# Decoder trunk on one core: the page loop's softmax steps set further apart, and the expert layers' first weight halves and exponentials moved earlier

## The reference

```
def page_step(carry, p_idx):
    ckv = pool_ckv[page_table[:, p_idx]]
    s = mla_scores(q_nope, q_pe, mla_keys(ckv, w_uk, kn_nope), pool_kpe[phys])
    return merge(carry, s, ckv), None          # running softmax, values = p @ ckv
```

```
q = (xb @ w_q).reshape(PEER_BLOCK, PEER_HEADS, 2, PEER_D_KEY // 2)
s = einsum('thcd,cnd->thcn', q, sub_keys)      # 8 heads, two halves, 128 keys each
s1, i1 = top_k(s[:, :, 0], 16); s2, i2 = top_k(s[:, :, 1], 16)
top_s, top_pos = top_k(s1[..., :, None] + s2[..., None, :], 16)
gate = softmax(top_s); act = gelu(u_tab[experts] . xb)
return sum(gate * act * v_tab[experts])
```

## Time and profile before

| | before |
|---|---|
| median of 3 timed runs | 3015.54 us (3010.78 to 3016.44) |
| the profiled execution's own time | 3003.13 us |
| its span in the profile | 3001.5 us |
| TensorE busy | 2789.8 us, 93% of the span |
| VectorE, ScalarE, GpSimd busy | 62%, 43%, 7% |
| mean granted TensorE clock | 0.949 of 2.4 GHz |
| query loops of the two expert layers | about 383 to 450 us, 2120 to 2187 us |
| experts | about 453 to 1252 us, 2190 us to the end |
| page loop | about 1411 to 2050 us; the first 16 pages carry the prompt's 16 heads too |

### The profile page before, as it was taken

One profiled execution on the slowest core, in us unless ns is written; L12 is line 12 of the kernel. 1 busy time (PEld: TensorE's weight loads), 2 busy tenths in 40 slices (PEclk: granted clock), 3 DMA queues, 4 the chain that ended last, 5 costly groups with the idle time before them and its releaser, 6 DMA issues.

```text
span 3001.5 us, 59707 instructions
## 1 busy us (share of the span) xinstructions
PE 2789.8 (93%) x22390; PEld 2577.9 (86%) x22390; DVE 1864.9 (62%) x3534; ACT 1292.3 (43%) x2607; POOL 221.0 (7%) x319
## 2 busy tenths in 40 slices
PE   8977899999999999976989999998999999999998
PEld 5767689999999999845877777777899999999998
DVE  5566469989975555424654444442679899855554
ACT  2333124477764444311433333331244677644443
POOL 0044000000000000000022222221000000000000
PEclk9999999999999999986989998887999999999999
DMA  4311135444445555620122222221345444455553
GB/s 165 121 35 31 60 116 168 162 157 159 157 155 182 182 180 179 220 102 14 32 71 74 73 75 66 67 62 60 122 155 164 160 156 159 146 181 181 182 181 134
DMA packets 105660, 378.50 MB, mean 126 GB/s; under 512 B 14618, under 2 KB 14875, under 8 KB 104931
## 3 DMA queue, kind: packets, MB, share of 16 engines
q1 hardware_dynamic: 88562, 322.17, 32.4%
q0 software_dynamic: 16880, 53.42, 6.0%
HBM read 371.52 MB, written 4.01 MB: 125 GB/s over the span
## 4 chain that ended last, share of the span: by engine, by line
PE 87%; DVE 8%; issue 2%; ACT 2%; DMA 0%; DVEq 0%; POOL 0%; ACTq 0%; POOLq 0%; SPq 0%
PE ps L733 85%; DVE arena L1929 2%; DVE arena L1374 1%; ACT arena L2072 1%; DVE arena L1378 1%; PE ps L1032 1%; PE ps L1027 1%; DVE arena L1958 0%; DVE ring_lo L1374 0%; PE ps L792 0%; DVE arena L1951 0%; DVE arena L1939 0%; ACT w_hi L2072 0%; DVE arena L1932 0%; DVE arena L1892 0%
## 5 line engine op out<-in xcount | busy, mean ns | idle before, releaser
L1374 DVE TENSOR_TENSOR ring_lo<-ring,w_hi 128x1024 fp32r<-128x1024 f32 x512 | 625.4, 1223 | 418.0 <-ACT w_hi L2072 413.5
L2072 ACT ACTIVATE arena<-ps 128x256 f32<-128x256 f32 (+18 forms) x981 | 396.9, 424 | 964.5 <-PE ps L733 886.4
L2072 ACT ACTIVATE w_hi<-ring 128x1024 fp32r<-128x1024 f32 x512 | 541.8, 1059 | 391.4 <-PE ps L733 391.1
L733 PE MATMUL ps<-x_hi,w_hi 128*128 128x264 f32 x2048 | 595.5, 291 | 15.5 <-DVE ring_lo L1374 15.5
L733 PE MATMUL ps<-h_hi,w_hi 128*128 128x264 f32 x2048 | 580.5, 283 | 6.8 <-DVE ring_lo L1374 6.8
L733 PE MATMUL ps<-x_hi,ring_lo 128*128 128x264 f32 x2048 | 585.0, 286 | 0.0
L733 PE MATMUL ps<-x_lo,w_hi 128*128 128x264 f32 x2048 | 584.8, 286 | 0.0
L733 PE MATMUL ps<-h_lo,w_hi 128*128 128x264 f32 x2048 | 582.7, 285 | 0.0
L733 PE MATMUL ps<-h_hi,ring_lo 128*128 128x264 f32 x2048 | 582.3, 284 | 0.0
L733 PEld LDWEIGHTS ps<-arena 64*64 64x64 f32 (+4 forms) x5452 | 440.8, 160 | 157.3 <-DVEq L1371 45.4
L733 PE MATMUL ps<-arena 64*64 64x64 f32 (+11 forms) x5452 | 483.0, 252 | 89.1 <-DVEq L1371 49.7
(11 more groups left out here) (154 smaller groups left out, 2446.3 us busy)
## 6 DMA issues: line engine op xcount, KB each, us to landing
ring<-in_wstream SPq DMA_DIRECT2D x608, 512.0 KB, 3.3
arena<-in_cache_t POOLq DMA_DIRECT2D x128, 192.0 KB, 2.6
arena<-in_cache_n POOLq DMA_DIRECT2D x128, 128.0 KB, 2.3
arena<-in_mla_w POOLq DMA_DIRECT2D x1, 3072.0 KB, 10.2
arena<-in_state POOLq DMA_DIRECT2D x4, 512.0 KB, 4.4
out_wkv_s<-arena POOLq DMA_DIRECT2D x4, 512.0 KB, 4.1
arena<-in_consts SPq DMA_DIRECT2D x1, 1408.0 KB
arena<-in_consts POOLq DMA_DIRECT2D x1, 1408.0 KB, 13.8
```

The lines of the kernel that those rows point to most:

```text
L733: return nc.tensor.matmul(out, lhsT, rhs, start=start, stop=stop, **kw)
L1374: return v.tensor_tensor(out, a, b, op)
L2072: return nc.scalar.activation(out, in_, func, **kw)
```

## The change

All of it is a change of order; no instruction is added or taken away.

- **Page loop.** TensorE: `turn_max` goes from p=2 to 4, `spread_max` from 4 to 7, `prob_sums` from 7 to 10, the first values from p=7 to p=10. The rest of a request's values (pages 6 to 15) go two at a time in the next request's pages 0 to 4, none in pages 5 to 9. For the last-but-one request three go at each of p=10 to 14 and one at 15. VectorE: `spread_max` 2 to 4, `shift_scores` 4 to 7, `prob_sums` 6 to 9, `inverse_sums` 7 to 10, `request_out` 6 to 5. ScalarE: `request_probs` 5 to 8. GpSimd: row pages follow 14 behind the key pages instead of 12, and none beside key pages 20 and 21.
- **Expert layers.** ScalarE's first three `upper` calls (`WHI` = 3) go from behind the query loop into its tiles 13, 14 and 15. VectorE starts its `lower` calls ahead of head 5 instead of head 4 (the sixth head, counted from one). `EXP_AT` goes from 38 to 28.

```
-EXP_AT = 38
+EXP_AT = 28
...
             for n in range(20, PAGES):
                 page_keys(n)
-                page_rows(n - 12)
-            for n in range(PAGES - 12, PAGES):
+                if n >= 22:
+                    page_rows(n - 14)
+            for n in range(PAGES - 14, PAGES):
                 page_rows(n)
...
                 if q >= 0:
-                    if p == 2:
+                    if p == 4:
                         turn_max(q)
-                    if p == 4:
+                    if p == 7:
                         spread_max(q)
-                    if p == 7:
+                    if p == 10:
                         prob_sums(q)
-                if q >= 1 and p < 7 and req < NS:
-                    page_values(q - 1, p + 9)
-                if q >= 0 and p >= 7:
+                if q >= 1 and p < 5:
+                    page_values(q - 1, 6 + 2 * p)
+                    page_values(q - 1, 7 + 2 * p)
+                if q >= 0 and p >= 10:
                     if req < NS - 1:
-                        page_values(q, p - 7)
-                    elif p < 15:
-                        page_values(q, 2 * (p - 7))
-                        page_values(q, 2 * (p - 7) + 1)
+                        page_values(q, p - 10)
+                    else:
+                        for k in range(3 * (p - 10), min(3 * (p - 9), NPAGE)):
+                            page_values(q, k)
...
                     w.next(s_copied, 2)
-                    if h == PH // 2:
+                    if h == 5:
                         pace(WHI * PACE)
-                    choose_head(h, pace if h >= PH // 2 else no_pace)
+                    choose_head(h, pace if h >= 5 else no_pace)
...
                         tell(bank_free[b], s_copied)
+                    if 16 - WHI <= g < 16:
+                        upper(g - (16 - WHI))
...
-                for e in range(WHI):
-                    upper(e)
...
                 if q >= 0:
                     if p == 1:
                         root(of_req(SS, q))
-                    if p == 5:
+                    if p == 8:
                         request_probs(q)
```

More of the change, by code:

```diff
@@ L2029, in _ @@
                         request_scores(q)
-                    if p == 2:
+                    if p == 4:
                         spread_max(q)
-                    if p == 4:
+                    if p == 7:
                         shift_scores(q)
-                    if p == 6:
+                    if p == 9:
                         prob_sums(q)
-                    if p == 7:
+                    if p == 10:
                         inverse_sums(q)
-                if q >= 1 and p == 6:
+                if q >= 1 and p == 5:
                     request_out(q - 1)
@@ L2100, in peer, with upper @@
                 fn(x_hi[:, :], xnbuf).then_inc(xhi_ready, 1)
+                u0 = TILES[f"peer{layer}"]
+                def upper(e, it=0):
+                    n = u0 + e
+                    act.wait_ge(slot_in[n % RING], it * 48 + 16 * (n // RING + 1))
+                    if e >= WHI:
+                        act.wait_ge(tile_used, it * 15 + (n - WHI + 1))
+                    fn(upper_of(e), slot(n).rearrange("p c m -> p (c m)")).then_inc(hi_ready, 1)
                 for g in range(17):
@@ L2114, in peer @@
                 tell(bank_free[3], s_copied)
-                u0 = TILES[f"peer{layer}"]
                 s0, p0 = NSETS * layer, (P - LEAD_U) * layer
                 done = marks["done", layer]
[L2119 to L2125, removed]
                 def gelu(n):
```

## The result

The changed kernel takes 2924.35 us (median of 4 runs, 2912.70 to 2930.64) against 3013.16 us (4 runs, 2994.82 to 3016.44): ratio 0.971, 95% interval 0.966 to 0.976. The forecast was 2940, within 2914 to 2968. The profiled executions differ by 90.4 us (3003.13 and 2912.70 us; spans 3001.5 and 2911.0 us). The forecast gain was 75.

A forecast was written before the change was run, and what follows sets the result against it. The prediction took TensorE as the bound, losing time to waits and to 1.2 GHz after them. Page loop 47.0 + 0 + 4.5 = 51.5 and experts 23.6 made 75 us: from 3015.5 to 2940, range 2914 to 2968.

The forecast's parts named there:

- the wait at page 2: Page loop, TensorE's transpose of the maxima, requests 2 to 7: 22.5 us of waits and 24.5 of clock loss go, 47.0.
- The first request: Page loop: transpose wait replaced by 5.3 us for late key page 20, start 3.2 us earlier, clock loses it again: 0.
- The wait at page 10: Page loop, probability sums: 1.5 us wait moves from page 7 and stays; 1.3 us plus 3.2 of clock gained, 4.5.
- never: Rival: the clock never falls behind the wait at page 10; gain 95.6 us, time 2920; chance 17%.
- always: Rival: the clock always falls behind the wait at page 10; gain 56.6 us, time 2959; chance 13%.
- Pages with two and three values: Page loop: the same values per request, only placed otherwise; no gain or loss in sum, 0 us.
- the slower rival: Page loop: the clock doesn't recover in pages carrying two or three values; about 3235 us; chance 3%.
- Experts, start: Expert layers: the 3.18 us wait before the first expert and 1.7 us of half clock go, per layer.
- Exponentials and turn: Expert layers: 4.58 us wait at expert 39, 1.9 of clock and the turn's 0.91 go, less 0.5, per layer.
- the 2 us by the page: Expert layers: by the skill page's table-switch cost, TensorE would wait about 1.1 us more per layer, 2 in all.

The follow-up runs named there:

- the repeat: The changed kernel run again with no edit: 2929.19 us.
- Key pages first: The changed kernel with no row pages issued ahead of key page 20, but two behind each of key pages 20 to 27: 2912.37 us.
- page loop only: The changed kernel with its expert edits taken back, leaving the page loop's and GpSimd's changes: 2942.23 us.
- transpose at page 2: The changed kernel with the transpose of the maxima and VectorE's reader of it back at page 2 instead of 4: 2968.47 us.
- both: The changed kernel with probability and inverse sums at page 11, and row pages issued behind key pages 20 to 27, none ahead: 2890.84 us.
- Early uppers: The changed kernel with exponentials back at expert 38 and lower halves ahead of head 4, upper halves still in the query loop: 2928.83 us.
- experts only: The kernel before with only the expert part of the change, page loop and row pages as before: 2990.50 us.

## Why the prediction was right

**What bounds, and the wait at page 2** (forecast 47.0). The mechanism held. The transpose waits nowhere but behind the loop, nothing stands at pages 3 to 5, and putting the step back costs 39 to 44 us, 19.9 of it waits. The size of the clock term was read too low if anything: 24.5 in that one trace, 30.7 in the experiment.

**The first request** (0). The wait for page 20 came as forecast, 5.35 us for 5.3, and page 20 starts 3.0 us earlier for 3.2. The clock took them back nearly whole, as forecast: of the 6.8 us at half clock 5.8 lie behind that start, and up to the sums of page 22 only 0.7 us were gained (1.5 in the repeat). "Key pages first" shows that 8.0 us more lay there.

**The wait at page 10** (4.5). The wait came in all seven, at 1.48 us. The clock loss behind it, for which I took 20.5 us (2.55 x 6 + 5 is 20.3), was mis-sized: 10.2 / 2 = 5.1 in the profiled execution, 11.9 in the repeat, (4 x 6.8 + 10.2) / 2 = 18.7 in "page loop only". The 5 us for the last request were right (5.1); the 15.3 for the other six were 0 and 6.8 in the two executions. The count of falls was taken from one trace, and of a kernel in which each such wait came about 25 us behind a longer one; whether that mattered isn't shown. Between "never" and "always" the truth moves from run to run: counted from 3008 us, where the study's runs of before lie, they are 2912 and 2951, and the two medians, 2924 and 2929, lie between. In the profiled executions this term gave 15.4 us more than forecast and the first request 0.7; the page loop as a whole gave 66 for 51.5, so 2 us of it went elsewhere, 0.7 of them in the first 16 pages.

**Pages with two and three values** (0). Right: the requests are even at 64.8 us, and the slower rival, a clock that stays down there, didn't show in the changed kernel. It exists in small: in "transpose at page 2" one fall under two values a page lasted 20.5 us. Without a wait ahead of them, in "both", those pages stay at 1.00.

**Experts, start** (4.9 a layer). Right. Three upper halves fit into ScalarE's pauses, the first lower half was done at about 443.1 and TensorE ready at about 443.5. "Early uppers" shows that this part hangs on ScalarE alone.

**Exponentials and turn** (6.48 + 0.91 - 0.5). The waits at both went. The price was 1.4 us instead of 0.5, since three waits came and not one. The whole expert part gave 10.3 us a layer in the traces instead of 11.8, but measured alone only 14.0 us for both layers. The Trainium skill, ScalarE: Activation LUTs, section "What ACT_TABLE_LOAD costs", gives about 2.66 us per switch; two switches and three exponentials again took 529.97 - 526.75 = 3.2 us, so the measurement decides, and the 2 us by the page didn't come.

**The sum.** By the table the waits and work fell by 34 (2846 to 2812), forecast 22.5 + 1.3 + 16.3 = 40; the clock gave 47 to 50, forecast 24.5 + 3.2 + 7.2 = 35. The two errors partly cancel, and so do those of the parts: the page loop alone gave 64 us for 51.5, the experts alone 14.0 for 23.6. The mechanisms held, but that 75 came out as 77.5 in the same group of runs is in part luck. The rest of the distance from 2940 is the starting point: 3015.5, from which I subtracted, was the median of 3 runs, and the study's runs of before have medians of 3004.5 to 3009.8. From 3008, 75 would have given 2933.

The parts measured alone, 64 and 14, add up to 78, against 77.5 to 89 for the whole.

## What to carry to other kernels

A short wait of the bounding engine is worth its own length plus what the clock loses behind it, and here the second was the larger part (by the table 46 of 81 us, within one group of runs): where waits recur in a loop, set the step late enough that the engine never stands, rather than shorten the stand. A wait left over is worth removing even at 1.5 us, since all seven gave 21 to 26 us with their falls (17.9 in the traces). And count falls of the clock over several executions, by span times granted clock of every run; in one trace a wait with a fall and one without look alike until the row of the windows view behind them.

## What the runs showed of the hardware that was not expected

- The same wait of 1.48 us, at the same instruction of the same program, was followed by 6.8 to 10.2 us at 1.2 GHz in one of seven requests in one execution and in three of seven in another; in the last request it was so in all eight traces, in the others in 15 of 48; 3.3 to 3.9 us at the transpose was followed by a fall in all 18 cases of three kernels (requests 2 to 7).
- How long a fall lasts differs for the same wait: 3.4, 13.7, 20.5, 6.8, 6.8 and 10.2 us behind six transposes that waited 3.3 us each.
- The unchanged page loop of "experts only" lost 10 us more in its profiled execution than in that of before, with 126 us at 1.2 GHz for 109. These are one execution of each, so that the falls depend on the stage ahead isn't shown.
